# The second layer's modulation product moved out of the SSD scan and into the out projection

## The reference, cut to what matters

```python
silu_c, silu_cc = jax.nn.silu(c), jax.nn.silu(c_ctx)
for l in range(2):
    sh1, sc1, g1, sh2, sc2, g2 = jnp.split((silu_c @ ada_w[l] + ada_b[l])[:, None, :], 6, axis=-1)
    csh1, csc1, cg1, csh2, csc2, cg2 = jnp.split(silu_cc @ ada_w[l] + ada_b[l], 6)
    a_l = modulate(rmsnorm(h, norm1_w[l]), sh1, sc1)      # x * (1 + scale) + shift
    a_c = modulate(rmsnorm(hc, norm1_w[l]), csh1, csc1)
    out_l, out_c = ssd_mixer(a_l, a_c, ...) if l == 0 else attn_mixer(a_l, a_c, ...)
    h = h + g1 * out_l                                    # hc likewise with cg1 in layer 0
    m_l = modulate(rmsnorm(h, norm2_w[l]), sh2, sc2)
    h = h + g2 * grouped_moe(m_l, ...)                    # hc likewise in layer 0
```

## Time and profile before

| what | value |
|---|---|
| median of 3 runs | 1557.12 us (1556.64 to 1557.83) |
| the profiled execution, its own time | 1554.12 us |
| its span in the profile | 1552.2 us |
| mean granted PE clock | 0.966 |
| PE busy | 1416.5 us (91%), 12332 matmul records |
| DVE busy | 529.4 us (34%) |
| ACT busy | 385.9 us (25%) |
| POOL busy | 188.6 us (12%) |

### The profile page before, as it was taken

One profiled execution on the slowest core, in us unless ns is written; L12 is line 12 of the kernel. 1 busy time (PEld: TensorE's weight loads), 2 busy tenths in 40 slices (PEclk: granted clock), 3 DMA queues, 4 the chain that ended last, 5 costly groups with the idle time before them and its releaser, 6 DMA issues.

```text
span 1552.2 us, 28858 instructions
## 1 busy us (share of the span) xinstructions
PE 1416.5 (91%) x12332; PEld 810.3 (52%) x12332; DVE 529.4 (34%) x954; ACT 385.9 (25%) x949; POOL 188.6 (12%) x213
## 2 busy tenths in 40 slices
PE   5999889999988999979999998998999989999884
PEld 2543445455545544435556655654756766655442
DVE  2544655545443221144122211115255351222112
ACT  2311334233333320030122221213044211222111
POOL 0000134224142210000011111000000001111100
PEclk9799999999999999989999999999999999999987
DMA  9364434344332352102999999994330349999993
GB/s 369 112 201 154 136 109 142 103 136 139 133 109 82 82 135 81 54 4 86 404 405 390 382 382 383 393 330 161 122 109 1 125 159 371 395 397 399 401 405 139
DMA packets 130260, 334.46 MB, mean 215 GB/s; under 512 B 13203, under 2 KB 63051, under 8 KB 123979
## 3 DMA queue, kind: packets, MB, share of 16 engines
q1 hardware_dynamic: 117739, 308.02, 54.3%
q0 software_dynamic: 6144, 12.60, 2.3%
q10 hardware_dynamic: 6240, 11.90, 2.1%
HBM read 325.65 MB, written 14.68 MB: 219 GB/s over the span
## 4 chain that ended last, share of the span: by engine, by line
PE 69%; SPq 15%; DMA 7%; DVE 4%; ACT 2%; issue 2%; DVEq 0%; POOLq 0%; ACTq 0%
SPq L547 11%; PE ps L1159 11%; PE ps L1467 8%; PE ps L1176 7%; PE ps L1371 7%; PE ps L1421 4%; PE ps L1506 4%; SPq L549 3%; PE ps L1102 3%; PE ps L1264 2%; PE ps L1765 2%; PE ps L1531 2%; PE ps L1677 2%; DMA tmp<-in_ada_w 2%; PE ps L1251 2%
## 5 line engine op out<-in xcount | busy, mean ns | idle before, releaser
L1159 PE MATMUL ps<-aT,ring 128*128 128x512 f32 x384 | 175.7, 607 | 0.0
L1467 PE MATMUL ps<-ring,ssb 128*32 128x256 f32 x2224 | 134.5, 383 | 5.8 <-DMA ring<-in_moe_w_up 4.1
L2179 DVE COPY big<-ps 32x256 f32<-32x256 f32 x160 | 67.7, 423 | 146.9 <-PE ps L1506 145.2
L1159 PEld LDWEIGHTS ps<-aT,ring 128*128 128x128 f32 x384 | 71.9, 194 | 84.3 <-issue 84.3
L1176 PE MATMUL ps<-aT,ring 128*128 128x512 f32 x256 | 114.2, 595 | 0.0
L1371 PE MATMUL ps<-big,ring 128*128 128x512 f32 x256 | 110.2, 592 | 0.0
L1467 PEld LDWEIGHTS ps<-ring,ssb 128*32 128x32 f32 x2224 | 82.2, 111 | 51.7 <-DMA ring<-in_moe_w_up 8.0
L2170 DVE TENSOR_TENSOR ssb<-ssb,ps 128x256 f32<-128x256 f32 (+1 forms) x53 | 18.6, 355 | 256.1 <-ACT ssb L960 256.1
L1467 PE MATMUL ps<-tmp,ssb 128*32 128x256 f32 x1728 | 100.2, 379 | 4.0 <-DMA tmp<-in_moe_w_up 4.0
L867 ACT ACTIVATE ssb<-ps,ncum 128x128 f32<-128x128 f32 x256 | 73.1, 371 | 97.2 <-PE ps L1239 96.4
L1421 PE MATMUL ps<-aT,ring 128*128 128x512 f32 (+1 forms) x256 | 87.9, 500 | 6.8 <-ACT aT L795 6.8
(11 more groups left out here) (388 smaller groups left out, 1860.7 us busy)
## 6 DMA issues: line engine op xcount, KB each, us to landing
ring<-in_ada_w SPq DMA_DIRECT2D x44, 1024.0 KB
ring<-in_moe_w_down SPq DMA_DIRECT2D x40, 1024.0 KB
ring<-in_moe_w_gate SPq DMA_DIRECT2D x56, 512.0 KB
ring<-in_moe_w_up SPq DMA_DIRECT2D x56, 512.0 KB
tmp<-in_moe_w_gate SPq DMA_DIRECT2D x48, 512.0 KB
tmp<-in_moe_w_up SPq DMA_DIRECT2D x48, 512.0 KB
ring<-in_ssd_in_w SPq DMA_DIRECT2D x20, 1024.0 KB
tmp<-in_moe_w_down SPq DMA_DIRECT2D x16, 1024.0 KB
```

The costliest lines, as they stand in the source:

```text
L1159: ins = pe.matmul(ps[:, bank, :], slot(u)[:, k, (i % 2) * P:(i % 2 + 1) * P], aT[:, k, :], start=(k == 0), stop=(k == KD - 1))
L1467: ins = pe.matmul(tiled_gu[32 * c:32 * c + 32, 2 * h + i, :].rearrange("p (r n) -> p r n", r=2), XgT[l][:, k * C + 32 * g:k * C + 32 * g + ...
L2179: ins = dve.tensor_copy(Y[s % 2][32 * g:32 * g + 32, 256 * c:256 * c + 256], tiled_y[32 * c:32 * c + 32, 2 * h + i, :])
```

## The change

PE no longer multiplies the units of layer 1. While PE runs the out projection, DVE and ACT scale each unit's 128x2048 tile by the vectors' values per partition, and DVE and POOL add the eight units of a q up elementwise in SBUF. DVE takes all 2048 columns for the first vector and columns 0 to 511 for the second (`ada_part`); ACT scales columns 512 to 2047 for the second (`ada_scaled`) and POOL adds them (GpSimd, into `asum[1]`). PE then sums over the partitions with a matrix of ones (`ada_sum`), three times: within m = 2, within m = 4 and after m = 6; `ada_turn` of q = 3 to 5 follows after m = 2, after m = 4 and within m = 7. `ada_part` of four units stands on DVE ahead of the work of each m = 0 to 5, and `ada_scaled` of four on ACT ahead of the square of each k = 0 to 5. SP loads the units late, into four slots of their own: unit i when unit i - 4 has been used by DVE and ACT. The diff, without two renamed semaphores:

```diff
 ADA_QL = ADA_Q // 2
+ADA_PE = ADA_QL * KD
 AMOD_N = {(0, 0): 1, (0, 1): 2, (1, 0): 3, (1, 1): 4}
...
         uses.append(("BK", n // 4 + 1))
-    if n % 4 == 1:
-        uses.append(("ada", n // 4 + 2))
+    if n == 1:
+        uses.append(("ada", 2))
     return uses
...
 B4 = {use: j for j, use in enumerate(u for n in range(-1, STEPS) for u in bank4_uses(n))}
-B3 = {use: j for j, use in enumerate(u for n in range(-1, STEPS) for u in bank3_uses(n))}
+B3_MIXER = [u for n in range(-1, STEPS) for u in bank3_uses(n)]
+B3 = {use: j for j, use in enumerate(B3_MIXER + [("ada", q) for q in range(ADA_QL, ADA_Q)])}
...
+    if name == "ada" and v >= ADA_PE:
+        return (SLOTS, SLOTS + 1, SLOTS + MORE, SLOTS + MORE + 1)[v % 4]
     if name == "ada":
...
     for n in range(STEPS + 4):
-        i, ada = n + AHEAD, [("ada", KD + AHEAD + 2 * n + r) for r in range(2)] if n < 13 else []
+        i, ada = n + AHEAD, [("ada", KD + AHEAD + 2 * n + r) for r in range(2)] if n < 1 else []
         early += ada[0:1] + [("xbc", i // 2)] * (i < NCONV and i % 2 == 0)
...
     order = early + [("out", v) for v in range(KD)]
-    places = [(name, early_slot(name, v), 16) for name, v in early]
+    places = [(name, early_slot(name, v), 16) for name, v in early + [("ada", v) for v in range(ADA_PE, ADA_Q * KD)]]
     places += [("out", (EARLY_SLOTS + j) % SLOTS, 16) for j in range(KD)]
...
         wx = [spare[:, 2064 + 512 * n:2576 + 512 * n] for n in range(2)]
-        arow = spare[:, 3088:3600]
+        arows = [spare[:, 3088:3600]] * ADA_QL + [tmp[:, 4096:4608]] * ADA_QL
+        vsel = ssb[:, 4096:4160]
+        scaled = [ssb[:, 4160:5696], tmp[:, 6144:7680]]
+        asum = [ssb[:, 2048 * v:2048 * v + 2048] for v in range(2)]
...
+        def ada_summed(i):
+            return ADA_PE + i // KD * (KD + 1) + i % KD + 1
         def dense_free(l, e, j):
...
                     sp_.wait_ge(s_b4, B4["st", NG - 1, 5] + 1)
-                    sp_.wait_ge(s_b3, B3["ada", ADA_Q - 1] + 1)
+                    sp_.wait_ge(s_b3, B3["ada", ADA_QL - 1] + 1)
                 fetch(name, v)
...
+            def shared_unit(l, name, j0, j):
+                u = units[name][j]
+                sp_.wait_ge(*held[u.slot])
+                weights(u, j0 + j, a["shared_w_gate"][l], a["shared_w_up"][l], a["shared_w_down"][l])
+                held[u.slot] = unit_free(name, j)
+            def ada_late(first, last):
+                for i in range(first, last):
+                    if i >= 4:
+                        sp_.wait_ge(s_ada, ada_summed(i - 4))
+                        sp_.wait_ge(s_ha, 4 + i - 3)
+                    elif i == 0:
+                        sp_.wait_ge(s_dtx, 2 * STEPS)
+                        sp_.wait_ge(s_wx, 6 * NG)
+                        sp_.wait_ge(s_offv, 6 * NG)
+                    fetch("ada", ADA_PE + i)
             def shared(l, name, j0):
-                for j, u in enumerate(units[name]):
-                    sp_.wait_ge(*held[u.slot])
-                    weights(u, j0 + j, a["shared_w_gate"][l], a["shared_w_up"][l], a["shared_w_down"][l])
-                    held[u.slot] = unit_free(name, j)
+                for j in range(len(units[name])):
+                    shared_unit(l, name, j0, j)
...
-                shared(l, f"sgu{l}", 0)
                 if l:
+                    shared(l, f"sgu{l}", 0)
                     sp_.wait_ge(s_kv, 3)
...
             for name, v in order:
+                if name == "out":
+                    ada_late(*((0, 0), (0, 0), (0, 4), (4, 4), (4, 4), (4, 4), (4, 8), (8, 12))[v])
                 load(name, v)
+            ada_late(12, 16)
+            shared_unit(0, "sgu0", 0, 0)
+            ada_late(16, 19)
+            shared_unit(0, "sgu0", 0, 1)
+            ada_late(19, 24)
+            shared_unit(0, "sgu0", 0, 2)
+            shared_unit(0, "sgu0", 0, 3)
             moe(0, order1)
...
                     weighted(g + (i == 3), 5)
+            pool.memset(vsel, 0.0).then_inc(s_set, 1)
+            pool.wait_ge(s_set, 11)
+            for v in range(2):
+                pool.memset(vsel[:, 33 * v:33 * v + 1], 1.0).then_inc(s_set, 1)
+            for i in range(ADA_PE):
+                pool.wait_ge(s_ha, 4 + i + 1)
+                if i % KD:
+                    pool.wait_ge(s_set, 13 + i)
+                    pool.tensor_tensor(asum[1][:, 512:2048], asum[1][:, 512:2048], scaled[i % 2], ALU.add).then_inc(s_set, 1)
+                else:
+                    if i:
+                        pool.wait_ge(s_ada, ada_summed(i) - 1)
+                    pool.tensor_copy(asum[1][:, 512:2048], scaled[i % 2]).then_inc(s_set, 1)
...
-            norm_modulate(0, 1, T, 3, lambda k: act.wait_ge(s_h1, k + 1))
+            def ada_scaled(i):
+                u, k = units["ada"][ADA_PE + i], i % KD
+                arrived(act, u)
+                if i >= 2:
+                    act.wait_ge(s_set, 13 + i - 1)
+                act.activation(scaled[i % 2], room[u.slot][:, 512:2048], ACT.Copy, scale=cs[:, k, 1:2]).then_inc(s_ha, 1)
+            def ready1(k):
+                for i in range(4 * k, min(4 * k + 4, ADA_PE)):
+                    ada_scaled(i)
+                act.wait_ge(s_h1, k + 1)
+            norm_modulate(0, 1, T, 3, ready1)
             moe_act(0)
...
                 bank3_free(("ada", q))
+                if q == ADA_QL:
+                    pe.wait_ge(s_rsy, 2)
                 for c in range(4):
-                    ins = pe.transpose(ps[:, 3, c * P:(c + 1) * P], arow[:, c * P:(c + 1) * P], ident)
+                    ins = pe.transpose(ps[:, 3, c * P:(c + 1) * P], arows[q][:, c * P:(c + 1) * P], ident)
                 ins.then_inc(s_b3, 1)
+            def ada_sum(q):
+                i = (q - ADA_QL + 1) * KD - 1
+                pe.wait_ge(s_ada, ada_summed(i))
+                pe.wait_ge(s_set, 13 + i + 1)
+                pe.wait_ge(s_row, q)
+                for v in range(2):
+                    for j in range(4):
+                        ins = pe.matmul(ps[32 * j:32 * j + 32, 2, :], vsel[:, 32 * v:32 * v + 32], asum[v][:, 512 * j:512 * j + 512],
+                                        start=(v == 0), stop=(v == 1))
+                ins.then_inc(s_ada, 1)
...
                     turn_x(n + 13)
-                if n < 13:
+                if n < 1:
                     ada_unit(KD + AHEAD + 2 * n)
...
                     z_chunk(n - 4, 0, 4)
-                if n < STEPS and n % 4 == 1:
-                    ada_turn(n // 4 + 2)
+                if n == 1:
+                    ada_turn(2)
                 if early:
...
                     rows_per_head(n + 1, DIRS[(n + 1) % 4][0])
-                if n < 13:
+                if n < 1:
                     ada_unit(KD + AHEAD + 2 * n + 1)
...
                     ins = pe.matmul(ps[:, 4 + m % 4, :], w[:, k, :], xT[:, k, :], start=(k == 0), stop=(k == KI - 1))
+                    if (m, k) in ((2, 7), (4, 7)):
+                        ada_sum(m // 2 + 2)
+                    if (m, k) == (7, 7):
+                        ada_turn(5)
                 ins.then_inc(s_op, 1)
+                if m in (2, 4):
+                    ada_turn(m // 2 + 2)
+                if m == 6:
+                    ada_sum(5)
                 if m == 0:
                     pe.wait_ge(s_ssq, KI)
-                    pe.wait_ge(s_b3v, len(B3))
+                    pe.wait_ge(s_b3v, len(B3_MIXER))
                     pe.matmul(ps[:, 3, :], mean[:, :], ssq[:, :], start=True, stop=True).then_inc(s_rsy, 1)
             pe.wait_ge(s_rw, 5)
+            pe.wait_ge(s_b3v, len(B3))
...
-                dve.wait_ge(s_ada, KD * (q + 1))
+                dve.wait_ge(s_ada, KD * (q + 1) if q < ADA_QL else ada_summed((q - ADA_QL + 1) * KD - 1) + 1)
                 if q:
                     dve.wait_ge(s_b3, B3["ada", q - 1] + 1)
-                dve.tensor_copy(arow, ps[:, 2, :]).then_inc(s_row, 1)
+                dve.tensor_copy(arows[q], ps[:, 2, :]).then_inc(s_row, 1)
+            def ada_part(i):
+                u, k = units["ada"][ADA_PE + i], i % KD
+                arrived(dve, u)
+                if i:
+                    dve.wait_ge(s_ada, ada_summed(i) - 1)
+                for s, w, c in ((asum[0], room[u.slot], cs[:, k, 0:1]), (asum[1][:, 0:512], room[u.slot][:, 0:512], cs[:, k, 1:2])):
+                    if k:
+                        ins = dve.scalar_tensor_tensor(out=s, in0=w, scalar=c, in1=s, op0=ALU.mult, op1=ALU.add)
+                    else:
+                        ins = dve.tensor_scalar(s, w, c, None, ALU.mult)
+                ins.then_inc(s_ada, 1)
...
                 takes = [use for use in bank4_uses(n) if use[0] != "R"] if step else []
-                if n % 4 == 1 and step:
-                    ada_rows(n // 4 + 2)
+                if n == 1:
+                    ada_rows(2)
                 if n >= 5:
...
                     conv(n + AHEAD)
-                if n % 4 == 1 and step:
```

(18 more changed lines are left out.)

## The result

The changed kernel takes 1619.98 us (median of 4 runs, 1613.76 to 1621.83) where the kernel before took 1557.47 beside it. The ratio is 1.0393, with a 95% interval from 1.0363 to 1.0422: slower by 3.9%. The profiled execution took 1613.76 us, 59.6 more than that of before; the prediction had 1612.4 for it and 1615.4 for the median. The other three executions took 1619 to 1622 us, and what their 6 us more are no profile here shows.

A forecast was written before the change was run, and what follows sets the result against it. PE alone was taken to bound the out projection, with DVE and POOL, locked against each other, delaying it after the change. 1554.1 - 13.5 + 71.8 = 1612.4, plus 3.0 gives a 1615.4 us median; range 1594 to 1632, opened by 2 below.

The forecast's parts named there:

- Part 1, the scan: Scan on PE: losing 24 units and three transposes gains 13.5 us, bounds 9 and 19 us.
- The count by place: Scan: each removed unit saves only what PE would not then wait for ACT, 0.1 to 1.0 us or nothing.
- the lower clock: PE in the scan: a gain of up to 19 us if the lower clock goes as well.
- Part 2, the durations: Out projection, eight units: DVE 22.7 us, POOL 26.3 us; ACT's scaling at most 2.2 us each.
- The lock: Out projection: DVE and POOL exclude each other at the shared port, so times add to 48.5 us for eight units.
- an exception of the first unit of a q: Out projection, DVE: `ada_part` has two SBUF inputs in all but this unit, a plain product of 1.9 us.
- The times of the three sums: Out projection, PE: sums done at 618.5, 671.0 and 723.5, the stretch ending at 738.4, 71.8 us longer.
- The waits of PE: Out projection: PE stands 23, 20 and 13 us before the three sums.
- The router's preparation on POOL: After POOL's adds: 140 us later than before, but 1.5 us long and ended before 725.
- The one without the lock: Rival, out projection: port is no bound, POOL alone sets the first sum, later waits hidden; 1567 us, chance 12%.
- The faster one: Rival, out projection: PE never waits at the first sum, POOL needing 1.7 us a unit; 1551 us, chance 5%.
- The round trip of slots: Rival, out projection: slot, scaling and add leave the port idle, another 20 us, 1635 us; chance 7%.

The follow-up runs named there:

- the run of the scan alone: Changed kernel with layer 1's product, loads, sums and transposes left out and its modulation set to constants; 1547.85 us, ratio 0.9941 to the kernel before.
- the run with POOL's writes: Changed kernel with each POOL add replaced by three memsets that read nothing, POOL kept as busy; 1572.6 us, ratio 1.0121 to the kernel before.

## Why the prediction was right

**Part 1, the scan.** 13.5 us predicted, 12.6 measured in the profiled execution; 9.2 by the run of the scan alone. The count by place holds: the steps 1 to 4 gained 4.3 us together (predicted 4.5); step 7, where both units should pay 2.0, gained 2.3 us (27.4 to 25.1), step 5 0.7 (predicted 0.75), step 8 1.3 (1.15), step 10 1.3 (1.1), the steps 11 and 12 together 2.1 (2.0), and step 13 nothing. The term that was mis-sized is the lower clock. The prediction let it only add ("19 us if the lower clock goes as well"); step 14, where it had nothing, lost 1.6 us to it.

**Part 2, the durations.** DVE's 2048 columns take 2.35 us alone (predicted 2.29), its 512 columns 0.75 (0.68), POOL's add 3.45 (3.41), and the starts of adds that stand alone are 3.6 apart (3.5). ACT's scaling takes 1.56, below the bound of 2.2.

**The lock** was the large term, and it is as stated: their times add. By the profile of before it rested on one pair of operations; the experiments show it by taking away first the adds and then only their reading. What the Trainium skill says (SBUF — State Buffer, Who interferes with whom), that a VectorE instruction with two SBUF inputs contends with a GpSimd one that reads SBUF and not with one that only writes, the two runs bear out with 2351 ns beside memsets and 3341 to 4017 beside adds. The prediction made an exception of the first unit of a q, whose plain product has one SBUF input, and yet put its 1.9 us into the sum. The sum was right to have it: that product too stood behind POOL, beside an add (3.65 us) and even beside a memset (1.68 us).

**The times of the three sums**, from the start of the projection: the first at 58.8 us (predicted) and 56.8 (measured), then from sum to sum 52.5 (predicted) and 53.2 to the second, 52.5 and 53.4 to the third, 18.9 and 19.0 to the end; in all 182.7 and 182.4. The waits of PE were put at 23, 20 and 13 us and are 21.5, 21.7 and 14.4. A sum at the lower clock takes 3.4 to 3.6 us, not 4.0. The close agreement is in part luck, since smaller misses cancel. From the end of the first sum to the second DVE spent 45.6 us in `ada_part` and behind POOL's adds, where 46.9 were predicted, and 3.9 us on its other work, where 1.6 were.

**Wrong in the detail.** The prediction had DVE and POOL alternate through each stretch, with either one ending it. In fact POOL rests for 10.8 us in the second and in the third stretch, and DVE ends all three:

```profile
613.14 5.29 POOL L759 TENSOR_TENSOR ssb<-ssb,tmp 128x1536 f32<-128x1536 f32 x1
629.26 4.84 POOL L759 TENSOR_TENSOR ssb<-ssb 128x1536 f32<-128x1536 f32 x1 [10.82 <-ACT ssb L1079]
```

ACT's next scalings are queued behind the square of m = 2 (in the third stretch, of m = 4), which waits for DVE's residual add, which stands behind four `ada_part`. I had not followed that queue. By my reading it changed nothing in the sum, because DVE had work of its own in the gap and ran it at full speed; with POOL as the slower engine it would have. No run shows either. The router's preparation on POOL was put at 1.5 us and took 6.1 (700.45 to 706.55), its operations standing behind DVE's; nobody waited for it.

**The rivals.** The one without the lock (1567) is the run with POOL's writes, at 1572.6. The faster one needed POOL at 1.7 us a unit; it takes 3.4. The round trip of slots never left DVE idle but once, 4.7 us for the load of unit 4.

## What to carry to other kernels

Add up the times of VectorE operations with two SBUF inputs and of GpSimd operations that read SBUF. Don't take it that one input makes a VectorE operation safe: the plain product here has one, and was held by an add and by a memset. What the experiments showed side by side is a VectorE operation with two SBUF inputs and a GpSimd memset. Before taking work off a busy engine, look at each place for what the next instruction there would wait for: of 24 us of matmuls the scan gave back 12.6 in one execution and 9.2 by the run of the scan alone. And ask which part of a product is read at all: dropping the two thirds of the second vector's product that nobody reads, and moving the sums to where their input is ready, took this design from 1.0202 with VectorE alone to 0.9968.

## What the runs showed of the hardware that was not expected

- A DVE operation with two SBUF inputs (`scalar_tensor_tensor`) runs at its own pace beside GpSimd memsets of the same tile: 2351 and 744 ns, against 2351 and 747 beside an idle POOL.
- A DVE `tensor_scalar` with one SBUF tile to read is held where those with two inputs are not: 512 columns took 1.68 us beside a memset and 3.65 beside an add, against 0.47 with nothing beside it.
- Short GpSimd operations are hit hardest: a copy of 128 columns behind `ada_part` took 1.99 us where it takes 0.29 in the kernel before.
- Emptying an engine's stream can come with new stretches at the lower clock: step 14 of the scan, with the same work in both kernels, took 15.73 us at a granted clock of 1.00 before and 17.34 at 0.90 after.
- What a wait cost PE by the lower clock did not grow with its length: the 16 records of a sum took 3.49 us after a wait of 4.11 us and 3.40 after one of 21.48, against 1.92 at the full clock. The 16 records behind them took 7.13 us in both cases, as at the full clock, and up to 8.15 behind other waits.
